# Loading the input by feature halves in a two-layer-block kernel: the first product starts on four feature tiles, token squares and norm follow

## The reference

```python
h = rmsnorm(x, g_pre_mix)                       # x * rsqrt(mean(x*x) + eps) * gain
proj = jnp.einsum('bsd,de->bse', h, w_in)
u_pool = proj[..., :POOL_WIDTH]
qkv = proj[..., POOL_WIDTH:].reshape(B, S, 3, SB_HEADS, SB_HEAD_DIM)
```

## Time and profile before

| | |
|---|---|
| median of 3 runs | 1885.51 us (1885.04, 1886.6, 1885.51) |
| profiled execution, span | 1883.8 us |
| PE busy | 1861.2 us, 99% of the span |
| DVE busy | 1165.4 us, 62% |
| ACT busy | 917.1 us, 49% |
| POOL busy | 75.4 us, 4% |
| DMA | 171.33 MB moved, mean 91 GB/s |

### The profile page before, as it was taken

The page is one execution under the profiler, slowest core; times in us unless marked ns, Lnnn a source line. Parts: engine busy times, 40 slices in busy tenths (PEclk is TensorE's granted clock), DMA queues, the critical chain, the costliest instruction groups (busy, mean ns, idle before and its releaser), DMA issues.

```text
span 1883.8 us, 27086 instructions
## 1 busy us (share of the span) xinstructions
PE 1861.2 (99%) x8985; PEld 1504.1 (80%) x8985; DVE 1165.4 (62%) x2030; ACT 917.1 (49%) x1685; POOL 75.4 (4%) x110
## 2 busy tenths in 40 slices
PE   8999999999999999999999999999999999999998
PEld 7888888888888877677888888888757878888887
DVE  6877765733333377776566666336777576666534
ACT  6777654543433353666544434334456553444433
POOL 1111000000000000100200000000010020000000
PEclk9999999999999999999999999999999999999999
DMA  5222232333333324521333333333441223333333
GB/s 153 69 79 79 76 104 79 101 95 100 95 98 97 95 73 102 108 53 35 101 95 95 95 95 105 96 95 88 118 83 43 68 81 109 95 95 95 96 95 106
DMA packets 169241, 171.33 MB, mean 91 GB/s; under 512 B 48563, under 2 KB 123329, under 8 KB 169153
## 3 DMA queue, kind: packets, MB, share of 16 engines
q1 hardware_dynamic: 169048, 170.16, 31.5%
q10 hardware_dynamic: 104, 0.03, 0.0%
HBM read 159.25 MB, written 2.10 MB: 86 GB/s over the span
## 4 chain that ended last, share of the span: by engine, by line
PE 91%; DVE 5%; ACT 2%; issue 1%; DMA 0%; SPq 0%; DVEq 0%; ACTq 0%
PE bank_b L2457 16%; PE bank_b L2458 16%; PE bank_b L2459 16%; PE bank_a L2457 11%; PE bank_a L2458 11%; PE bank_a L2459 11%; PE bank_b L2959 2%; PE bank_b L3063 2%; PE bank_a L3044 1%; DVE w_lo L1535 1%; DVE arena L1538 1%; DVE arena L1535 1%; PE bank_a L2482 1%; PE bank_a L2485 1%; PE bank_a L2488 1%
## 5 line engine op out<-in xcount | busy, mean ns | idle before, releaser
L1535 DVE TENSOR_TENSOR w_lo<-w_raw,w_hi 128x512 fp32r<-128x512 f32 (+2 forms) x621 | 412.3, 675 | 535.3 <-ACT w_hi L1264 327.4
L1264 ACT ACTIVATE w_hi<-w_raw 128x512 fp32r<-128x512 f32 (+3 forms) x396 | 232.9, 599 | 435.6 <-PE bank_b L2459 222.2
L2457 PE MATMUL bank_b<-h_hi,w_hi 128*128 128x512 f32 (+1 forms) x952 | 372.7, 391 | 1.9 <-DVE h_lo L1538 0.8
L2459 PE MATMUL bank_b<-h_hi,w_lo 128*128 128x512 f32 (+1 forms) x952 | 369.0, 388 | 0.0
L2458 PE MATMUL bank_b<-h_lo,w_hi 128*128 128x512 f32 (+1 forms) x952 | 369.0, 388 | 0.0
L901 ACT ACTIVATE w_hi<-w_raw 128x512 fp32r<-128x512 f32 x225 | 137.7, 627 | 227.6 <-PE bank_b L2459 116.9
L2457 PEld LDWEIGHTS bank_b<-h_hi,w_hi 128*128 128x128 f32 x952 | 178.8, 188 | 41.2 <-issue 3.1
L2458 PEld LDWEIGHTS bank_b<-h_lo,w_hi 128*128 128x128 f32 x952 | 178.8, 188 | 37.0 <-issue 1.4
L2459 PEld LDWEIGHTS bank_b<-h_hi,w_lo 128*128 128x128 f32 x952 | 178.7, 188 | 36.6
L2457 PE MATMUL bank_a<-h_hi,w_hi 128*128 128x512 f32 x513 | 200.6, 391 | 0.3
L2458 PE MATMUL bank_a<-h_lo,w_hi 128*128 128x512 f32 x513 | 199.5, 389 | 0.0
(11 more groups left out here) (314 smaller groups left out, 2665.3 us busy)
## 6 DMA issues: line engine op xcount, KB each, us to landing
w_raw<-in_w_up_dram SPq DMA_DIRECT2D x240, 256.0 KB, 3.1
w_raw<-in_w_down_dram SPq DMA_DIRECT2D x152, 256.0 KB, 2.6
arena<-arena SPq DMA_DIRECT2D x32, 268.0 KB, 4.2
w_raw<-in_w_in_dram SPq DMA_DIRECT2D x64, 128.0 KB, 2.3
w_raw<-in_w_gate_dram SPq DMA_DIRECT2D x32, 256.0 KB, 2.8
w_raw<-in_w_in_dram SPq DMA_DIRECT2D x32, 256.0 KB, 2.6
w_raw<-in_w_o_dram SPq DMA_DIRECT2D x32, 256.0 KB, 2.6
w_raw<-in_w_out_dram SPq DMA_DIRECT2D x16, 256.0 KB, 2.7
```

Source lines behind the costliest of these rows:

```text
L1264: nc.scalar.activation(w_hi[:, s, 0:c], w_raw[:, s, 0:c], ACT.Copy).then_inc(w_round, 1)
L1535: return nc.vector.tensor_tensor(out_, a, b, op)
L2457: nc.tensor.matmul(out_, a_hi, b_hi, start=start, stop=False, skip_group_check=loose)
L2459: return nc.tensor.matmul(out_, a_lo, b_hi, start=False, stop=stop, skip_group_check=loose)
```

## The change

The input is loaded by feature halves: first features 0 to 511 of all four token tiles (four DMAs of 256 KB), then chunk 0 of the weights, then features 512 to 1023 of all four, then chunk 1, then chunks 2 and 3. The four `x_land` semaphores now stand for half and pair of token tiles. PE turns feature tiles 0 to 3 first, does `fill(0)`, turns tiles 4 and 5, and goes on as before; the small vectors are turned in the middle of the first sixteen transposes. On ACT the squares, which need whole token tiles, move from ahead of chunk 0 to behind `input_hi(5)` (one) and behind `input_hi(7)` (three), and the root of the norm goes behind them. On DVE the steps of the norm move behind `input_copy(7)`, and `split_lo` of chunks 4 and 5 moves from behind the memsets to ahead of the copy that waits for the spread norm. On PE the spread of the norm moves from behind `fill(2)` to behind `fill(5)`. No arithmetic is added or taken away.

```diff
@@ -624,9 +624,11 @@
                         sp_.dma_start(dst[:, r, :].rearrange("p (b n) -> p b n", b=2),
                                       in_v[:, 2 * (n % 4) + r, pick, i, :]).then_inc(w_land[n % SLOTS], 8 * 2)
-            for t in range(TT):
-                sp_.dma_start(x_in[t], x_v[:, t, :].rearrange("p (a n) -> p a n", a=2)).then_inc(x_land[t], 16)
-            for k in range(SLOTS):
+            for half in range(2):
+                for t in range(TT):
+                    sp_.dma_start(x_in[t][:, half, :], x_v[:, t, half * HALF:half * HALF + HALF]).then_inc(x_land[2 * half + t // 2], 16)
+                load_fill(half)
+            for k in range(2, SLOTS):
                 load_fill(k)
             sp_.dma_start(consts[:, :], shape_consts).then_inc(pos_land, 16)
             sp_.dma_start(pos_i, positions.broadcast_to((P, S))).then_inc(pos_land, 16)
@@ -932,7 +934,7 @@
             def input_squares(t):
-                act.wait_ge(x_land[t], 16)
+                act.wait_ge(x_land[2 + t // 2], 32)
                 nc.scalar.activation(x_junk[t], x_in[t], ACT.Square, accum_out=tok[:, 0, t:t + 1]).then_inc(tok_sq, 1)
             def input_hi(f):
@@ -946,30 +948,30 @@
                 act.wait_ge(h_ready, f + 1)
                 nc.scalar.activation(x_t[:, f, :], x_bank(f), ACT.Copy).then_inc(xt_out, 1)
-            for t in range(3):
-                input_squares(t)
+            act.wait_ge(cols_out, 1)
             split1(0)
-            act.wait_ge(cols_out, 1)
             input_hi(0)
             input_hi(1)
-            input_squares(3)
             split1(1)
             input_hi(2)
             input_hi(3)
             input_copy(0)
             input_copy(1)
-            act.wait_ge(in_step, 1)
-            nc.scalar.activation(tok[:, 3, :], tok[:, 2, :], ACT.Ln).then_inc(in_guess, 1)
-            act.wait_ge(in_guess, 1)
-            nc.scalar.activation(tok[:, 4, :], tok[:, 3, :], ACT.Exp, scale=-0.5).then_inc(in_guess, 1)
             split1(2)
             input_hi(4)
             input_hi(5)
+            input_squares(0)
             input_copy(2)
             input_copy(3)
             split1(3)
             input_hi(6)
             input_hi(7)
+            for t in range(1, TT):
+                input_squares(t)
+            act.wait_ge(in_step, 1)
+            nc.scalar.activation(tok[:, 3, :], tok[:, 2, :], ACT.Ln).then_inc(in_guess, 1)
+            act.wait_ge(in_guess, 1)
+            nc.scalar.activation(tok[:, 4, :], tok[:, 3, :], ACT.Exp, scale=-0.5).then_inc(in_guess, 1)
             act.wait_ge(consts_made, 5)
             nc.scalar.activation(tri[:, :, :], tri_f, ACT.Copy).then_inc(tri_made, 1)
@@ -1639,11 +1641,8 @@
             split_lo(1)
             first_lo(2)
             first_lo(3)
-            dve.wait_ge(tok_sq, TT)
-            nc.vector.tensor_scalar(tok[:, 2, :], tok[:, 0, :], 1.0 / D, EPS, ALU.mult, ALU.add).then_inc(in_step, 1)
             split_lo(2)
             first_lo(4)
-            input_rstd()
             first_lo(5)
             input_copy(4)
             input_copy(5)
@@ -1652,6 +1651,11 @@
             first_lo(7)
             input_copy(6)
             input_copy(7)
+            dve.wait_ge(tok_sq, TT)
+            nc.vector.tensor_scalar(tok[:, 2, :], tok[:, 0, :], 1.0 / D, EPS, ALU.mult, ALU.add).then_inc(in_step, 1)
+            input_rstd()
+            for n in range(SLOTS, AHEAD - 2):
+                split_lo(n)
             dve.wait_ge(spread_in, 1)
             nc.vector.tensor_copy(rstd_in, bank_a[:, 2, :]).then_inc(rstd_spread, 1)
@@ -1720,8 +1724,6 @@
                 dve.wait_ge(v_round, i + 1)
                 rest(v_lo[i % 2], turned_v(b), v_hi[i % 2]).then_inc(vv_ready, 1)
-            for n in range(SLOTS, AHEAD - 2):
-                split_lo(n)
             dve.wait_ge(w_used, SLOTS)
             dve.wait_ge(rstd_spread, 1)
             take_out("qk", 0, 0)
@@ -2603,11 +2605,12 @@
                 return nc.tensor.transpose(x_bank(f)[:, t * P:t * P + P], x_in[t][:, f // 4, f % 4 * P:f % 4 * P + P], ident[:, :])
             for t in range(TT):
-                if t == TT - 1:
+                if t == 2:
                     pe.wait_ge(rows1_land, 16 * 6)
                     nc.tensor.transpose(bank_b[:, 0, 0:N_ROWS1], rows1, ident[0:N_ROWS1, 0:N_ROWS1]).then_inc(cols_made, 1)
-                pe.wait_ge(x_land[t], 16)
-                for f in range(FIRST_TURNED):
+                if t % 2 == 0:
+                    pe.wait_ge(x_land[t // 2], 32)
+                for f in range(4):
                     last = turn_input(f, t)
                     if t == TT - 1:
                         last.then_inc(xt_made, 1)
@@ -2702,13 +2705,20 @@
             for n in range(AHEAD - 1):
                 fill(n)
+                if n == 0:
+                    for f in range(4, FIRST_TURNED):
+                        for t in range(TT):
+                            if t % 2 == 0 and f == 4:
+                                pe.wait_ge(x_land[2 + t // 2], 32)
+                            last = turn_input(f, t)
+                        last.then_inc(xt_made, 1)
                 if n == 1:
                     for f in range(FIRST_TURNED, KT):
                         pe.wait_ge(xt_out, f - FIRST_TURNED + 1)
                         for t in range(TT):
                             last = turn_input(f, t)
                         last.then_inc(xt_made, 1)
-                if n == 2:
+                if n == 5:
                     pe.wait_ge(xt_out, 3)
                     pe.wait_ge(diag_in, TT)
                     nc.tensor.matmul(bank_a[:, 2, :], ones[:, :], rstd_diag, start=True, stop=True).then_inc(spread_in, 1)
```

## The result

The changed kernel takes **1894.05 us** (median of 5 runs, 1893.64 to 1895.9); the kernel before, on the same chip, 1885.71 (5 runs, 1885.04 to 1886.6). The ratio is 1.0049, with a 95% interval of 1.0038 to 1.0059: slower by 8.3 us, where 3.7 was predicted, and above the top of the range (1891.4). The span of the profiled execution grew from 1883.8 to 1892.3.

The account below looks back on a forecast made before the run. PE was taken as the bound, busy 99% of the span, so only its waits could shift time. Chunk 4 at -0.9 and chunk 6 at +4.5 gave +3.7 us: 1885.5 + 3.7 = 1889.2, range 1887.2 to 1891.4.

Parts of the forecast that it names:

- the line of operations on DVE: Behind the product of ones: copy, two memsets, two take-outs, then chunk 6's rest; chunk 6 starts 3.7 us later.
- ACT's chain: ACT's gapless work from chunk 1's landing, with three squares and the root, until chunk 4 starts on PE: 13.5 us.
- chunk 1 lands at 10.5: Opening loads: 2 KB rows of x at 380 GB/s instead of 398 put chunk 1 at 10.5 us, range 10.2 to 11.1.
- SP's four more DMAs: On SP ahead of the constants, some 0.5 us each; they fit in before chunk 4's load and cost nothing.
- the prediction's estimate from it: Opening loads at the skill's 341 GB/s: x would take 6.15 us and the result be 0.6 us worse.
- rival 2: Clock falls in the hole ahead of chunk 6, products behind it at half pace: +5.7 us, 1891.2; chance 0.12.
- Rival 3: No hole ahead of chunk 6, which follows the product of ones directly: -0.4 to -1.9 us, 1884.4; chance 0.05.
- narrow margin: Behind chunk 6, DVE's q and k splits are done about when PE finishes: no new wait, by 0.2 us.
- lead of the opening: First product at about 9.3 us instead of 11.61, 2.3 us earlier; 0.9 of it left at chunk 4.

Follow-up runs that it names:

- the experiment with the filled holes: Changed kernel plus 9 matmuls of no use ahead of chunk 4 and 15 behind the product of ones, so PE works through both waits: 1891.08 us, ratio 1.0029.
- the experiment with the rests ahead of the copy: Changed kernel with DVE's rests of chunks 6 and 7 made ahead of the copy that waits for the spread norm: 1891.56 us, ratio 1.0037.

## Why the prediction was wrong

The direction and the place were right, and the line of operations on DVE that makes most of the forecast. The size was not: 8.3 us instead of 3.7. Two steps failed: chunk 1 landed late, so that chunk 4 was 1.6 us later than before and not 0.9 earlier, and the clock fell, which the sum has at nothing. Term by term:

| Step | predicted | measured |
|---|---|---|
| chunk 0 there | 6.6 | 8.32 |
| first product | 9.3 | 10.59 |
| chunk 1 there | 10.5 | 12.69 |
| ACT, chunk 1 to chunk 4 on PE | 13.5 | 13.75 |
| chunk 4 on PE | 24.0 | 26.44 |
| chunk 4 to the product of ones | 5.53 | 7.15 |
| product of ones to chunk 6 | 4.52 | 4.44 |
| chunk 6 on PE | 34.05 | 38.03 |
| chunk 6 to chunk 7 | 2.89 (33.28 less 30.39) | 4.33 |

Of the miss, 2.2 us come from chunk 1 and 0.25 from ACT's chain; the slow stretches add 1.6 and 1.4; the line on DVE takes back 0.1. That makes 5.4 at chunk 7 (9.1 where 3.7 was predicted), and 4.8 at the end. The 0.6 us in between are taken in somewhere behind chunk 7, and where was not settled.

**The step that failed first: "chunk 1 lands at 10.5".** It has two parts. The working went by the stores at the end for the rate of 2 KB rows (380 GB/s), because they were the nearest row. They are stores, long after the start, with nothing beside them; the loads of the opening moved at 258 GB/s from 2.2 to 7.7 us where whole rows moved at 371. And it counted SP's four more DMAs only against chunk 4 ("nothing"), though they stand ahead of chunk 1's loads as well, which were handed out 2.0 us later (6.24 against 4.26). Whether the rate or the later start holds the landing back, and what made the rate low, stays open: the change did reach 352 GB/s with the same rows from 8.25 to 9.5 us, and the two versions that hand out chunk 1's loads ahead of the second half average 309 and 317 GB/s over the same ten slices (2.2 to 7.7 us). The term was bounded at 11.1 from above, and it measured 12.69. In the five traces with the change's own order of loads it was 12.69, 12.87, 11.73, 12.21 and 12.02 us: also in the best of them it is above that bound. The Trainium skill, DMA: Bandwidth & Descriptors, section Bandwidth, gives 341 GB/s at 1 MB; the prediction's estimate from it, 0.6 us more, erred the same way and less. The rate from 2.2 to 7.7 us was lower still than that figure, which is for DMAs four times as large. The cut of the loads alone cost the kernel before 1.2 us in the median, and what share the order of the loads has in the rest was not separated.

**The second: the clock was taken to hold (rival 2, at 0.12), and its fall stood in the sum at nothing.** The prediction read from the earlier trace rows that the clock holds for over 4 us without a product, and judged a hole of 3.5 by it. That was one observation at the end of the program, and it did not carry over: the clock fell behind 3.41 us in all four traces that have this hole, behind 2.80, and in one of three traces with about 2.2. The price per hole, 1.6 and 1.4 us, was put at 2 for one, a little high; there were two. The Trainium skill, TensorE: Matmul & The Clock Gate, section HAM oscillation, warned of just this, a wait between groups of matmuls that starts the next group cold. The windows of the changed kernel agree, with 0.50 granted behind both waits (other versions show waits up to 2.26 us without a fall), and the experiment with the filled holes took the 0.50 away and 2.5 us with it.

**What held.** DVE's line behind the product of ones, each of its terms within 0.1 us; and ACT's chain within 0.25. Rival 3 (the hole is not there) was rightly low for the kernel as it stands, and the experiment with the rests ahead of the copy showed its mechanism, with a new wait of 2.26 us that the prediction had not named for it. The "narrow margin" behind chunk 6, that q and k would be in time for the scores, held also with chunk 6 at full pace: in the kernel without idle PE they start at 39.47 with no wait ahead of them. It is gone only where chunk 6 follows the product of ones directly. Of the lead of the opening, the prediction had 2.3 us at the first product and it was 1.0, and none of it reached chunk 4.

## What to carry to other kernels

An early start is worth only what the engine with the longest chain behind it can pass on: here ACT's chain led from the second weight chunk to the fifth, and the squares that were moved off the head of its list landed ahead of chunk 4, where they cost more than the start gave. Before a step that waits is moved on an engine's list, write down what stands behind it there and when each is due; the rest of chunk 6, five operations behind the wait for the spread, made PE stand for 3.4 us. Count also the DMAs that a cut of a load puts ahead of the next one on its queue's engine. And an idle stretch of TensorE may cost more than its length: behind 2.8 and 3.4 us TensorE went at half pace in every trace here, behind some 2.2 us in one of three, and each such stretch cost 1.3 to 1.6 us more; where such a stretch could not be removed, matmuls that nobody reads made it cheaper.

## What was not expected of the hardware

- The granted clock fell from 2.4 to 1.2 GHz behind holes of 3.41 us (four traces of four), 2.80 (one) and 2.23 (one), and did not behind 0.65, 1.08 (two traces), 1.75, 2.19 and 2.26, though it had held for over 4.4 us at the end of the kernel before. So between 2.19 and 2.26 us the same length went both ways, and the length of the hole alone does not decide. In the changed kernel each stretch at 1.2 GHz lasted some 3.4 us (27.2 to 30.6, and 37.4 to 40.8).
- Loads of 256 KB in 2 KB rows, cut from rows of 4 KB, moved, with the weights between or behind them, at 258 GB/s (the change) and 291 GB/s (the cut alone) over 2.2 to 7.7 us, whole rows at 371; with chunk 1 ahead of the second half it was 317. In the change the same rows then moved at 352 GB/s (8.25 to 9.5 us), so their length alone does not set the rate. The landing of chunk 1 differed by 1.1 us between executions with the same order of loads.
- Twenty-four matmuls added to the changed kernel made it 2.5 us faster.
